# Thirty-two tokens more in the gathered expert rounds of a two-block network, and a pair search over 65 places

## What is computed

```
def peer(hn, w_q, sub_keys, u_emb, v_emb):
    q = (hn @ w_q).reshape(B, T, PEER_HEADS, 2, PEER_HALF)
    s = jnp.einsum('bthpd,hpkd->bthpk', q, sub_keys)
    s_top, i_top = lax.top_k(s, PEER_TOPK)
    cand = s_top[..., 0, :, None] + s_top[..., 1, None, :]
    cand_idx = i_top[..., 0, :, None] * PEER_KEYS + i_top[..., 1, None, :]
    best, pos = lax.top_k(cand.reshape(B, T, PEER_HEADS, n_cand), PEER_TOPK)
    experts = jnp.take_along_axis(cand_idx..., pos, axis=-1)
    gates = jax.nn.softmax(best, axis=-1)
    ...
        u = u_emb[ec]
        a = jax.nn.gelu(jnp.einsum('nd,nkd->nk', xc, u))
        return jnp.einsum('nk,nkd->nd', gc * a, v_emb[ec])
```

## Time and profile before

| What | Value |
|---|---|
| median of 3 runs | 4530.31 us (4530.06 to 4531.76) |
| the profiled execution, its own time | 4530.32 us |
| its span in the trace | 4528.5 us |
| PE busy | 4418.6 us, 98% of the span |
| DVE busy | 2733.0 us, 60% |
| ACT busy | 1742.6 us, 38% |
| POOL busy | 720.8 us, 16% |
| HBM traffic | 573.10 MB read, 29.36 MB written |

### The profile page before, as it was taken

One profiled execution on the slowest core, in us unless ns is written; L12 is line 12 of the kernel. 1 busy time (PEld: TensorE's weight loads), 2 busy tenths in 40 slices (PEclk: granted clock), 3 DMA queues, 4 the chain that ended last, 5 costly groups with the idle time before them and its releaser, 6 DMA issues.

```text
span 4528.5 us, 61846 instructions
## 1 busy us (share of the span) xinstructions
PE 4418.6 (98%) x21997; PEld 3702.0 (82%) x21997; DVE 2733.0 (60%) x4435; ACT 1742.6 (38%) x2871; POOL 720.8 (16%) x767
## 2 busy tenths in 40 slices
PE   8999999999999999999999998899999899999999
PEld 7888888888888887888888886687667788888888
DVE  5436556454444436656454278754898877777777
ACT  3223634332232225444332233442226644444444
...
GB/s 130 100 97 87 95 84 37 66 98 97 101 95 93 102 91 86 103 50 43 93 93 98 97 94 77 1 131 56 82 86 156 266 298 299 304 295 299 299 304 262
DMA packets 91046, 605.13 MB, mean 134 GB/s; under 512 B 12832, under 2 KB 13216, under 8 KB 24288
## 3 DMA queue, kind: packets, MB, share of 16 engines
...
HBM read 573.10 MB, written 29.36 MB: 133 GB/s over the span
## 4 chain that ended last, share of the span: by engine, by line
PE 87%; DVE 4%; ACT 2%; issue 2%; DVEq 2%; DMA 1%; POOLq 1%; ACTq 0%; POOL 0%; SPq 0%
PE PB L193 25%; PE PB L195 24%; PE PB L194 24%; PE PB L2741 3%; PE PB L1003 2%; PE PB L1231 2%; PE PB L3030 2%; PE PB L993 1%; PE PB L3045 1%; ACT WH L3196 1%; PE PB L1244 1%; PE PB L2254 1%; POOLq L256 1%; DVE WL L3247 1%; DVE YG L3234 0%
## 5 line engine op out<-in xcount | busy, mean ns | idle before, releaser
L193 PE MATMUL PB<-XH,WH 128*128 128x512 f32 (+1 forms) x3288 | 1260.1, 383 | 21.1 <-DVE WL L174 13.6
L195 PE MATMUL PB<-XH,WL 128*128 128x512 f32 (+1 forms) x3288 | 1242.2, 378 | 0.0
L194 PE MATMUL PB<-XL,WH 128*128 128x512 f32 (+1 forms) x3288 | 1241.2, 378 | 0.0
L174 DVE TENSOR_TENSOR WL<-RAW,WH 128x1024 fp32r<-128x1024 f32 x520 | 637.3, 1267 | 480.4 <-ACT WH L166 458.7
L193 PEld LDWEIGHTS PB<-XH,WH 128*128 128x128 f32 x3288 | 619.4, 188 | 130.3 <-issue 20.9
L194 PEld LDWEIGHTS PB<-XL,WH 128*128 128x128 f32 x3288 | 619.4, 188 | 100.1 <-issue 2.2
L166 ACT ACTIVATE WH<-RAW 128x1024 fp32r<-128x1024 f32 x504 | 504.4, 1049 | 509.8 <-PE PB L195 481.7
L195 PEld LDWEIGHTS PB<-XH,WL 128*128 128x128 f32 x3288 | 618.4, 188 | 100.2
L254 POOL TENSOR_TENSOR SQ<-SQ 128x512 f32<-128x512 f32 x49 | 72.5, 1480 | 2567.8 <-ACT SQ L236 2546.1
L3247 DVE TENSOR_TENSOR WL<-RAW,WH 128x1024 fp32r<-128x1024 f32 x220 | 269.8, 1226 | 220.2 <-ACT WH L3196 219.8
L193 PE MATMUL PB<-WH,WGH 128*128 128x512 f32 x768 | 301.0, 392 | 8.4 <-DVE WGL L3263 8.4
...
## 6 DMA issues: line engine op xcount, KB each, us to landing
...
GM<-gate_matrix POOLq DMA_DIRECT2D x128, 160.0 KB, 3.3
...
GM<-gate_matrix POOLq DMA_DIRECT2D x128, 32.0 KB, 3.7
...
```

The source lines that it names most:

```text
L174: c.nc.vector.tensor_tensor(c.WL[p][:, cols], c.RAW[p][:, cols], c.WH[p][:, cols].bitcast(F32), ALU.subtract).then_inc(c.sem("w_split"), 1)
L193: c.nc.tensor.matmul(out, wh, xh, start=start, stop=False)
L194: c.nc.tensor.matmul(out, wh, xl, start=False, stop=False)
L195: return c.nc.tensor.matmul(out, wl, xh, start=False, stop=stop)
```

## The change

The number of dense tokens falls from 384 to 352 (DENSE). The 32 tokens that leave, the last of the third block, take their 128 picks by gathered rows, four picks of each in one round, so 32 rounds more: the rows of a round's 128 partitions are 4 shares (SHARES) of 32 tokens. The extra round belongs to every step n with n % 4 == 1 (ROUNDS, ROUNDS_OF). It has its own token rows XG2, picks IDX2, gates GP2 and sum YG2, and shares the three buffers UV. At the end, before the last product, PE adds YG2 into the third block's banks with a matrix SHARE that sums the four shares. The early activations, `act_in`, AG, WG and GM shrink to 352 columns; WGH and WGL stay 384 wide with zeros at the end. Gates has 88 groups, stored as four whole blocks and three halves. In choose, CAND holds 65 pairs of places, written by five additions, and shifts and masks turn a place back into two positions. XPK no longer shares CAND's memory, and HP lies in a part of a parameter table that is free by then.

```diff
-DENSE = DENSE_B * P
-OWN = slice(DENSE, S)
+EXTRA = 32
+SHARES = P // EXTRA
+DENSE = DENSE_B * P - EXTRA
+OWN = slice(DENSE_B * P, S)
+N_CAND = 65
...
-        V.tensor_tensor(c.CAND[:, :, :].rearrange("p t (a b) -> p t a b", a=TOPK),
-                        c.TV[:, 0, :, :].unsqueeze(3).to_broadcast([P, QB, TOPK, TOPK]),
-                        c.TV[:, 1, :, :].unsqueeze(2).to_broadcast([P, QB, TOPK, TOPK]), ALU.add)
+        for at, a, na, nb in CAND_PARTS:
+            V.tensor_tensor(c.CAND[:, :, at:at + na * nb].rearrange("p t (a b) -> p t a b", a=na),
+                            c.TV[:, 0, :, a:a + na].unsqueeze(3).to_broadcast([P, QB, na, nb]),
+                            c.TV[:, 1, :, 0:nb].unsqueeze(2).to_broadcast([P, QB, na, nb]), ALU.add)
...
+        last = c.nc.tensor.transpose(c.PB[:, 4 + k // 4, at], c.XG2[:, k * P:k * P + P], c.IDENT[:, :])
...
+        c.nc.scalar.activation(c.XG2[:, half * S:half * S + S], c.PB[:, 4 + half, :], ACT.Copy)
...
-BLOCKS = DENSE // TOK_BLOCK
+BLOCKS = DENSE // TOK_BLOCK - 1
+HALVES = DENSE // (TOK_BLOCK // 2) - 2 * BLOCKS
...
+ROUNDS = [(x, n // SHARES if x else n) for n in range(N_EXP) for x in ((False, True) if n % SHARES == 1 else (False,))]
+ROUNDS_OF = [[r for r, (x, m) in enumerate(ROUNDS) if (m * SHARES + 1 if x else m) == n] for n in range(N_EXP)]
+LAST_EXTRA = max(r for r, (x, _) in enumerate(ROUNDS) if x)
...
+        if x + 1 == len(PLAN):
+            pe.wait_ge(c.sem("pick_done"), LAST_EXTRA + 1)
+            for part in range(2):
+                c.nc.tensor.matmul(c.PB[:, 2 * DENSE_B + part, :], c.SHARE[:, :], c.YG2[:, part * S:part * S + S],
+                                   start=False, stop=False)
...
             V.memset(c.YG[:, :], 0.0)
+            V.memset(c.YG2[:, :], 0.0)
+            V.memset(c.SHARE[:, :], 0.0)
+            dve.drain()
+            for g in range(SHARES):
+                own = slice(g * EXTRA, g * EXTRA + EXTRA)
+                V.tensor_copy(c.SHARE[own, P - EXTRA:], c.IDENT[own, own])
...
-            pick_dot(STEPS_OF[x][0])
-        if len(tile) == 2:
+            pick_dot(rounds[0])
+        for r in rounds[1:]:
             dve.drain()
-            pick_dot(STEPS_OF[x][1])
-            pick_sum(STEPS_OF[x][0])
+            pick_dot(r)
+            pick_sum(r - 1)
             dve.drain()
...
-        if e >= 3:
-            pool.wait_ge(c.sem("pick_done"), e - 2)
-        pool.indirect_dma_start(c.UV[e % 3][:, :], None, rows,
-                                bass.IndirectOffsetOnAxis(ap=c.IDX[:, e:e + 1], axis=0))\
-            .then_inc(c.sem(f"rows_loaded{e % 3}"), 16)
+        for r in ROUNDS_OF[e]:
+            extra, n = ROUNDS[r]
+            picks = c.IDX2 if extra else c.IDX
+            if r >= 3:
+                pool.wait_ge(c.sem("pick_done"), r - 2)
+            pool.indirect_dma_start(c.UV[r % 3][:, :], None, rows,
+                                    bass.IndirectOffsetOnAxis(ap=picks[:, n:n + 1], axis=0))\
+                .then_inc(c.sem(f"rows_loaded{r % 3}"), 16)
```

More of the change, by code:

```diff
@@ L1892, in allocate2_arena @@
                 c.HS = [c.sb(f"HS{i}", [P, P], F32, q) for i in range(2)]
-                c.HP = [c.sb(f"HP{i}", [P, P], F32, q) for i in range(2)]
+                c.HP = [c.PR2[:, PRM2[n][0]:PRM2[n][0] + P] for n in ("dw_w", "cmp_w2k")]
                 c.STG = [stage, c.sb("STG1", [P, KEYS, TOK_BLOCK], F32, q)]
@@ L1897, in allocate2_arena @@
             c.AG, c.WG = c.sb("AG", [P, 2, DENSE], F32, s), c.sb("WG", [P, 2, DENSE], F32, s)
-            c.WGH, c.WGL = c.sb("WGH", [P, 2, DENSE], F32R, s), c.sb("WGL", [P, 2, DENSE], F32R, s)
+            c.WGH, c.WGL = (c.sb(n, [P, 2, DENSE_B * P], F32R, s) for n in ("WGH", "WGL"))
             c.GM = [c.sb(f"GM{i}", [P, DENSE], F32, s) for i in range(2)]
@@ L1901, in allocate2_arena @@
             c.YG, c.PRODG = c.sb("YG", [P, D], F32, s), c.sb("PRODG", [P, D], F32, s)
+            c.YG2, c.SHARE = c.sb("YG2", [P, D], F32, s), c.sb("SHARE", [P, P], F32, s)
             c.AV, c.CF = c.sb("AV", [P, 2], F32, s), c.sb("CF", [P, 2, 2], F32, s)
@@ L2885, in act_choose, with place_rows @@
     phase_end(c, act, cur)
+CAND_PARTS = [(16 * n, 2 ** n - 1, 2 ** n, 2 ** (4 - n)) for n in range(4)] + [(64, TOPK - 1, 1, 1)]
+def place_rows(c, m):
+    return c2(c, "iota")[:, 0:P:8] if m else c2(c, "iota")[:, 1:TOPK + 1]
 def dve_top16(c, dve, rows):
@@ L3063, in act_gates, with block @@
     hot(1, 1)
-    halves = c.STG[1][:, :, :].rearrange("p e t -> p (e t)").rearrange("p (h e t) -> p h e t", h=2, e=KEYS)
-    def block(i, s, early, last=False):
+    halves = [g[:, :, :].rearrange("p e t -> p (e t)").rearrange("p (h e t) -> p h e t", h=2, e=KEYS) for g in c.STG]
+    def block(i, s, early, split=False):
+        last = split and s == 1
+        groups = PER_BLOCK // 2 if last else PER_BLOCK
         act.wait_ge(c.sem(f"gm_stored{s}"), i * 16 + 16)
-        for q in range(PER_BLOCK):
+        for q in range(groups):
             half = q // DC
-            if last and q == PER_BLOCK - 1:
-                act.wait_ge(c.sem("gm_stored0"), BLOCKS // 2 * 16 + 16)
+            if last and q == groups - 1:
+                act.wait_ge(c.sem("gm_stored0"), STORED[0])
                 act_split(c, act, T_PEER, HEAD_P, L_EXPERTS // 2, (0,))
             act.wait_ge(c.sem("gm_full"), (i * 2 + s) * PER_BLOCK + (q + 3))
-            if not (last and q >= PER_BLOCK - 2):
+            if not (last and q >= groups - 2):
                 hot(q % 2, (i * 2 + s) * PER_BLOCK + (q + 2))
-            home = halves[:, half, :, q % DC * 4:q % DC * 4 + 4] if last else c.STG[s][:, :, q * 4:q * 4 + 4]
+            home = halves[s][:, half, :, q % DC * 4:q % DC * 4 + 4] if split else c.STG[s][:, :, q * 4:q * 4 + 4]
             c.nc.scalar.activation(home, tokens_inside(c, q % 2), ACT.Copy).then_inc(c.sem("gm_copied"), 1)
-            if last and q % DC == DC - 1:
+            if split and q % DC == DC - 1:
                 act.drain()
-                act.dma_start(last_halves(gm)[half], halves[:, half, :, :]).then_inc(c.sem("gm_stored1"), 16)
+                act.dma_start(last_halves(gm)[2 * s + half], halves[s][:, half, :, :])\
+                    .then_inc(c.sem(f"gm_stored{s}"), 16)
             if s == 0 and q == DC - 1:
@@ L3201, in gated_high, with pick_gain @@
             act.wait_ge(c.sem("y_done"), n)
-        A.activation(c.WGH[:, n % 2, :], c.WG[:, n % 2, :], ACT.Copy).then_inc(c.sem("wg_hi"), 1)
-    def pick_gain(n):
-        act.wait_ge(c.sem("pick_dot"), n + 1)
-        A.activation(c.CF[:, n % 2, 0:1], c.AV[:, n % 2:n % 2 + 1], ACT.Gelu_apprx_tanh)
+        A.activation(c.WGH[:, n % 2, :DENSE], c.WG[:, n % 2, :], ACT.Copy).then_inc(c.sem("wg_hi"), 1)
+    def pick_gain(r):
+        extra, n = ROUNDS[r]
+        gate = c.GP2 if extra else c.GP
+        act.wait_ge(c.sem("pick_dot"), r + 1)
+        A.activation(c.CF[:, r % 2, 0:1], c.AV[:, r % 2:r % 2 + 1], ACT.Gelu_apprx_tanh)
         act.drain()
-        A.activation(c.CF[:, n % 2, 1:2], c.CF[:, n % 2, 0:1], ACT.Copy, scale=c.GP[:, n:n + 1])\
+        A.activation(c.CF[:, r % 2, 1:2], c.CF[:, r % 2, 0:1], ACT.Copy, scale=gate[:, n:n + 1])\
             .then_inc(c.sem("pick_gain"), 1)
+    for W in (c.WGH, c.WGL):
+        A.activation(W[:, :, DENSE:], c.ONES[:, :2 * EXTRA].rearrange("p (s t) -> p s t", s=2), ACT.Copy, scale=0.0)
     for x, tile in enumerate(PLAN):
@@ L3223, in act_experts @@
         for n in STEPS_OF[x]:
-            pick_gain(n)
+            for r in ROUNDS_OF[n]:
+                pick_gain(r)
     A.activation(c.RR[:, 0:1], c.EPSC[:, 0:1], ACT.Sqrt)
@@ L3262, in gated_low @@
         dve.wait_ge(c.sem("wg_hi"), n + 1)
-        V.tensor_tensor(c.WGL[:, n % 2, :], c.WG[:, n % 2, :], c.WGH[:, n % 2, :].bitcast(F32),
+        V.tensor_tensor(c.WGL[:, n % 2, :DENSE], c.WG[:, n % 2, :], c.WGH[:, n % 2, :DENSE].bitcast(F32),
                         ALU.subtract).then_inc(c.sem("wg_split"), 1)
@@ L3266, in dve_experts @@
         more = x + 1 < len(PLAN)
+        rounds = [r for n in STEPS_OF[x] for r in ROUNDS_OF[n]]
         if more:
@@ L3270, in dve_experts @@
             dve.drain()
-            pick_dot(N_EXP - 1)
+            pick_dot(len(ROUNDS) - 1)
         gated(x, STEPS_OF[x][-1])
         if x:
-            pick_sum(STEPS_OF[x][0] - 1)
+            pick_sum(rounds[0] - 1)
         else:
             V.memset(c.YG[:, :], 0.0)
+            V.memset(c.YG2[:, :], 0.0)
+            V.memset(c.SHARE[:, :], 0.0)
+            dve.drain()
+            for g in range(SHARES):
+                own = slice(g * EXTRA, g * EXTRA + EXTRA)
+                V.tensor_copy(c.SHARE[own, P - EXTRA:], c.IDENT[own, own])
         gated_low(STEPS_OF[x][-1])
```

83 lines of the change are left out of this document (53 added, 30 removed).

## The result

The kernel after takes **4546.6 us** in the median of 7 runs (4545.0 to 4554.12), the one before 4530.94 (7 runs, 4527.74 to 4536.02). The ratio is 1.0036, 95% interval [1.0024, 1.0048]: slower by 16 us, where 8 us less was predicted. 4546.6 lies outside the range of 4511 to 4543.

A forecast was written before the change was run, and what follows sets the result against it. PE was taken to bound the kernel, at 87% of the chain that ended last. Terms -10.2 + 1.6 - 11.8 - 4.0 + 1.5 - 30.1 + 4.3 + 39.4 + 1.7 gave -7.6 us: 4523 us, 80% range 4511 to 4543.

The forecast's parts named there:

- Columns: PE matmuls 352 instead of 384 columns wide: 13.3 ns less each, -30.1 us in act_in and -10.2 in choose.
- Rival 3: In experts, narrower columns save nothing because the weight load sets the pace: 4546 us, chance 0.04.
- The search: In choose, DVE sheds over 20 us by searching 65 places, hidden behind PE's unbroken run: costed at nothing.
- Gates: In gates, 8 of 96 groups go, -11.8 us, and narrower early experts in the other 80 give -4.0 us.
- Start of experts: DVE's clears and corner copies between WG and WGL of the first step: +1.5 us on PE's path, bounds 0.9 and 2.5.
- The stalls of PE in experts: PE waits around pair steps: the standing stall grows by 4.3 us, and the 32 extra rounds add 39.4 us.
- s4: Last of five single steps in each period of seven; an extra round there costs 1.0 us, four times, +4.0 us.
- s0: First single step behind a pair; an extra round there costs 0.6 us, four times, +2.4 us.
- Rival 2: In experts, gathers land sooner and drains hide in ACT's wait, so stalls are 11 us less: 4512 us, chance 0.30.
- 2.85 x 9: Third round in nine pairs: 2.15 us from DVE's order plus 0.7 for a late third gather, +25.7 us in all.
- Rival 1: In experts, extra traffic makes transfers land 1 us later at 17 places without slack: +17, 4540 us, chance 0.24.
- Theory A: Follow-up theory for experts: extra rounds cost by their place in DVE's order, and slowly clocked matmuls follow a long stall.
- B: Follow-up theory for experts: 32 MB more traffic makes transfers late, wherever the extra rounds stand.

The follow-up runs named there:

- moved: The changed kernel with the same 32 extra rounds at other steps, never in a pair or the two single steps ahead of one: 4511.84 us, ratio 0.9953.
- pairs_all: The changed kernel with an extra round in the first step of all 17 pairs, the other 15 in second single steps: 4581.25 us, ratio 1.0109.

## Why the prediction was wrong

The stalls that the extra rounds cause were forecast within 3 us (39.4, measured 42.0), and the time still came out 24 us higher (4546.6 against 4522.7). Point by point, by the prediction's own steps:

- **Columns.** Right. Choose -9.5 (-8.6). In experts the kernel without rounds takes 897.4 us from first product to last matmul against 923.5: -26.1, where -30.1 + 4.3 + 1.7 = -24.1 was predicted. Between starts of act_in's matmuls there are 0.161 us in place of 0.174, the 13 ns that were taken. Rival 3, columns that give nothing, named 4546 us and so hit the measured time to a microsecond; that is chance, since the columns gave all that the sum had for them.
- **The search.** Right: no effect.
- **Gates.** 8 groups fewer gave -11.8, as predicted. The early activations gave 3.4 by themselves, but in the whole change the stretch grew by 1.7. This is the first miss, 5.7 us. It lies at the first store (2.3 us) and in the usual group (1.53 us in place of 1.49); the cause of neither is known. Another 0.8 is lost between the last group and the first `act_in`.
- **Start of experts.** +2.8 in place of +1.5, beyond the bound of 2.5: two memsets, four copies and their drains took the whole time between WG and WGL. With the clears elsewhere it is 0.
- **The stalls of PE in experts.** Nearly right. Predicted: 6.3 + 4.3 + 2.0 + 5.3 = 17.9 ahead of pairs; measured 20.1. Predicted behind pairs 4.0 + 25.7 = 29.7; the row of waits has 29.7, and start-to-start distances give 32.2 for the same places, so the equal figure is partly chance. By these distances the nine pair rounds took 28.6 (the order 2.06 each in place of 2.15, the late gather 1.1 in place of 0.7), s4 3.6 in place of 4.0 and s0 0.5 in place of 2.4. Rival 2, smaller stalls, is out.
- **What the step "2.85 x 9" left out.** It took a stall's cost to be its length. Behind the longer stalls PE's matmuls ran at the lower clock level, which cost 12.3 us by the windows. By the stretch's sum it is 12.7: 952.1 less 897.4 is 54.7, of which stalls are 56.0 - 14.0 = 42.0. This is the main failed step: the sum had no line for the clock, though the first step of the stage, where PE waits before its first product, ran slowly clocked in the trace of before as well (0.83 from 3580 to 3600). The Trainium skill has this cost ("TensorE: Matmul & The Clock Gate", "HAM oscillation — how this bites in real kernels"): waits between bursts of matmuls can turn the clock down each time, and the price is half of the slow time. The trace agrees: 0.41 x 4.0 = 1.6 us are lost behind the stall at 4043, in a slow stretch of 3.4. I had not applied it, since before the change PE waited no longer than 0.7 us behind the first step of this stage.
- **Rival 1 (late transfers by traffic)** named 4540, near the result, for the wrong reason: with all the traffic and no work the kernel takes 4497, and ACT's wait for weights is 2.0 us. Only its part on the third gather is real, and a fourth buffer removes it. Its limit was too low as well: it took 365 GB/s for a full share of the DMA engines, and stretches of 4 us in the kernel after moved 402 and 424 (windows above).

The miss in the two traces is 22.4 us (+14.8 against -7.6): clock 12.7, gates 5.7, start and barrier 2.1, stalls 2.6, less 0.9 in choose and 2.0 in columns, and 2.2 of scatter ahead of choose. Theory A holds: of four kernels that tell it from B all four went its way. Its sizes held to 8 us at moved (7.8) and pairs_all (7.3), and it gave the fourth buffer 8 us where 15.6 were measured. That excess isn't settled.
